# The inverse root of eleven norms in columns: squares as stationary operand, root and reciprocal on 128x4, four matmuls to spread the result over a bank

## The reference

```python
def layer_norm(x, g, b):                       # "a" (512 channels) and "x" (1024) in both layers
    mu = jnp.mean(x32, axis=-1, keepdims=True)
    var = jnp.mean(jnp.square(x32 - mu), axis=-1, keepdims=True)
    y = (x32 - mu) * lax.rsqrt(var + LN_EPS)
    return y * g + b

def rms_norm(x, g):                            # "q" (384), "kv" (256) in both layers; n0, n1, nf (1024)
    return x32 * lax.rsqrt(jnp.mean(jnp.square(x32), axis=-1, keepdims=True) + RMS_EPS) * g

a = jax.nn.silu(layer_norm(a, ln_a_g, ln_a_b))                     # branch A, behind its convolution
q = jnp.einsum("bsr,rk->bsk", rms_norm(q_lat, q_norm_g), w_uq)     # branch C
kv = jnp.einsum("bsr,rk->bsk", rms_norm(kv_lat, kv_norm_g), w_ukv)
return layer_norm(DEEPNORM_ALPHA * x + gate[:, None, :] * out, ln_g, ln_b)   # the end of a layer
```

## Time and profile before

| | us |
|---|---|
| median of 3 executions | 2508.64 (2507.86 to 2511.62) |
| profiled execution, whole | 2511.03 |
| its span on the core | 2509.2 |
| PE busy in it | 2302.8 (92%) |
| VectorE, GpSimd, ScalarE busy | 1454.2, 1070.8, 858.9 |
| mean granted clock of PE | 0.963 of 2.4 GHz |

### The profile page before, as it was taken

How to read it: one execution, slowest core, us unless ns; L and a number is a source line. 1 busy time by engine, 2 the same in 40 slices (tenths; PEclk the granted TensorE clock), 3 DMA queues, 4 the chain that set the end, 5 groups by cost and what they waited for, 6 DMA issues and landing times.

```text
span 2509.2 us, 30799 instructions
## 1 busy us (share of the span) xinstructions
PE 2302.8 (92%) x10776; PEld 1869.3 (74%) x10776; DVE 1454.2 (58%) x2336; ACT 858.9 (34%) x1394; POOL 1070.8 (43%) x1276
## 2 busy tenths in 40 slices
PE   6799899999799989999967989888999999899997
PEld 3587777888568777788746878777778778688875
DVE  5889976432478997632268373654766666423311
ACT  2332234222433233422244233333443443333211
POOL 1555435565246543555414342442343443344333
PEclk9999999999899999999988999999999999999999
DMA  8343324443223222333412222222243242122221
GB/s 294 120 143 110 109 89 139 146 155 118 93 97 111 91 80 78 112 126 107 136 30 86 76 89 86 74 91 98 84 143 112 82 143 81 58 70 73 76 67 67
DMA packets 93203, 259.80 MB, mean 104 GB/s; under 512 B 10128, under 2 KB 11536, under 8 KB 92944
## 3 DMA queue, kind: packets, MB, share of 16 engines
q1 hardware_dynamic: 71392, 210.23, 26.4%
q10 hardware_dynamic: 21680, 47.79, 5.3%
HBM read 237.01 MB, written 20.97 MB: 103 GB/s over the span
## 4 chain that ended last, share of the span: by engine, by line
PE 49%; issue 19%; DVE 15%; POOL 13%; ACT 3%; ACTq 1%; POOLq 0%; DMA 0%; DVEq 0%; SPq 0%
PE bank L1852 15%; PE bank L1853 15%; PE bank L1854 15%; POOL t L387 13%; DVE t L1551 4%; DVE t L1348 2%; DVE t L1067 1%; DVE t L1063 1%; PE bank L1935 1%; DVE t L1126 1%; PE bank L2212 1%; PE bank L1922 1%; DVE t L1548 1%; DVE t L1071 1%; POOL t L404 0%
## 5 line engine op out<-in xcount | busy, mean ns | idle before, releaser
L387 POOL TENSOR_TENSOR t<-t,t 128x256 fp32r<-128x256 f32 x1224 | 1030.2, 872 | 1270.1 <-ACT t L423 1269.7
L1852 PE MATMUL bank<-t,t 128*128 128x512 f32 (+2 forms) x3072 | 1196.9, 390 | 96.2 <-POOL t L387 26.9
L1853 PE MATMUL bank<-t,t 128*128 128x512 f32 (+2 forms) x3072 | 1167.8, 380 | 0.0
L1854 PE MATMUL bank<-t,t 128*128 128x512 f32 (+2 forms) x3072 | 1165.5, 379 | 0.0
L1852 PEld LDWEIGHTS bank<-t,t 128*128 128x128 f32 x3072 | 593.8, 193 | 229.7 <-DVE t L1063 22.9
L1853 PEld LDWEIGHTS bank<-t,t 128*128 128x128 f32 x3072 | 593.4, 193 | 108.5 <-issue 5.0
L1854 PEld LDWEIGHTS bank<-t,t 128*128 128x128 f32 x3072 | 591.1, 192 | 109.0
L423 ACT ACTIVATE t<-t 128x1024 fp32r<-128x1024 f32 x306 | 321.5, 1054 | 248.4 <-PE bank L1854 193.5
L1126 DVE SCALAR_TENSOR_TENSOR t<-t,t,t 128x512 f32<-128x512 f32 x168 | 162.8, 982 | 119.1 <-DMA t<-w_ada 96.2
L1348 DVE SCALAR_TENSOR_TENSOR t<-t,t,t 128x512 f32<-128x512 f32 x240 | 201.7, 840 | 6.7
L1067 DVE SCALAR_TENSOR_TENSOR t<-t,bank 128x512 f32<-128x512 f32 x112 | 76.7, 684 | 186.3 <-PE bank L1854 88.9
(11 more groups left out here) (229 smaller groups left out, 1685.8 us busy)
## 6 DMA issues: line engine op xcount, KB each, us to landing
t<-blocks SPq DMA_DIRECT2D x306, 512.0 KB, 3.7
t<-w_ada SPq DMA_DIRECT2D x144, 256.0 KB, 2.7
t<-w_ada SPq DMA_DIRECT2D x20, 512.0 KB, 11.6
xm_park<-t ACTq DMA_DIRECT2D x16, 384.0 KB, 2.3
s_park<-t ACTq DMA_DIRECT2D x16, 384.0 KB, 2.3
t<-xm_park ACTq DMA_DIRECT2D x16, 384.0 KB, 4.6
t<-s_park ACTq DMA_DIRECT2D x16, 384.0 KB, 5.0
xc_park<-t ACTq DMA_DIRECT2D x16, 256.0 KB, 2.0
```

Source lines behind the costliest of these rows:

```text
L387: low = pool.tensor_tensor(w_lo[slot][:, part], w_raw[slot][:, part], w_hi[slot][:, part].bitcast(F32), ALU.subtract)
L1852: pe.matmul(out, wh, xh, start=start, stop=False)
L1853: pe.matmul(out, wh, xl, start=False, stop=False)
L1854: return pe.matmul(out, wl, xh, start=False, stop=stop)
```

## The change

In the eleven norms the squares become the stationary operand and a column of ones the moving one. A matmul with 128 tokens of a square tile as its weights then gives the sum of each of these tokens in a partition of its own, one column; four of them a tile fill 128x4 of a bank. A matmul with zeros writes these four columns first. ScalarE takes the root of 128x4 and VectorE its reciprocal in `rstd`. Four matmuls, with a column of `rstd` broadcast to 128x128 as weights and the identity moving, write the 512 values into all partitions of a bank, and VectorE's multiplies read that bank. Where the root needs another table than what stands before it, a root of one spare column stands ahead of the squares (`root_ahead`). In a, `merge_gate(0, 0)` now stands behind the root; n0's sums go to bank 4 in place of 5.

```diff
+            def root_ahead():                       # ScalarE: ahead of the squares of a, x, n1, nf
+                act.activation(spare[:, 0:1], eps_rms[:], ACT.Sqrt).then_inc(act_done, a())
+
+            def column_std(bank, n, eps, ready, label):
+                act.wait_ge(pe_done, P(*ready))
+                act.activation(rstd[:], banks[bank][:, 0:4], ACT.Sqrt, bias=eps[:], scale=1.0 / n).then_inc(act_done, a(*label))
...
+                root_ahead()
                 for j in range(NA):
...
+                column_std(3, WA, eps_ln, (l, "a_sq", NA - 1), (l, "a_std"))
                 merge_gate(0, 0)
-                act.wait_ge(pe_done, P(l, "a_sq", NA - 1))
-                act.activation(tmp[2][:], banks[3][:], ACT.Sqrt, bias=eps_ln[:], scale=1.0 / WA).then_inc(act_done, a(l, "a_std"))
                 merge_gate(0, 1)
...
+            def column_rstd(std, label):            # VectorE
+                wa(*std)
+                dve.reciprocal(rstd[:], rstd[:]).then_inc(dve_done, d(*label))
...
             def x_norm(l, j):
-                dve.tensor_tensor(x[:, j, :], x[:, j, :], tmp[2][:], ALU.mult).then_inc(dve_done, d(l, "x_norm", j))
+                dve.tensor_tensor(x[:, j, :], x[:, j, :], banks[5][:], ALU.mult).then_inc(dve_done, d(l, "x_norm", j))
...
                 rotate(tmp[2][64:96, :], banks[1], l, "k_rope")
+                column_rstd((l, "kv_std"), (l, "kv_rstd"))
                 products(B_UQ(l))
...
+            def sum_columns(bank, tile, n, j, label):           # PE
+                if j == 0:
+                    pe.matmul(banks[bank][:, 0:4], ident[:], zeros[:], start=True, stop=False)
+                for t in range(4):
+                    mm = pe.matmul(banks[bank][:, t:t + 1], tile[:, 128 * t:128 * (t + 1)], ones[:, 0:1], start=False, stop=(j == n - 1 and t == 3))
+                mm.then_inc(pe_done, p(*label))
+
+            def spread_rows(bank, ready, label):
+                pe.wait_ge(dve_done, Dn(*ready))
+                for t in range(4):
+                    mm = pe.matmul(banks[bank][:, 128 * t:128 * (t + 1)], rstd[:, t:t + 1].to_broadcast([128, 128]), ident[:], start=True, stop=True)
+                mm.then_inc(pe_done, p(*label))
...
                 for j in range(3):
                     pe.wait_ge(act_done, A(l, "q_lat_sq", j))
-                    sum_rows(banks[2], tmp[j % 2][:], 3, j, (l, "q_sq", j))
+                    sum_columns(2, tmp[j % 2], 3, j, (l, "q_sq", j))
...
+                spread_rows(3, (l, "q_rstd"), (l, "q_rows"))
                 pe.wait_ge(act_done, A(l, "kv_lat", 0))
                 u_chunk(banks[1], B_KR(l), (l, "k_rope"))
...
+                    if h == 0:                      # behind the first q head
+                        spread_rows(6, (l, "kv_rstd"), (l, "kv_rows"))
...
-                    sum_rows(banks[3], tmp[j % 2][:], NA, j, (l, "a_sq", j))
+                    sum_columns(3, tmp[j % 2], NA, j, (l, "a_sq", j))
+                pe.wait_ge(act_done, A(l, "exp", 31))
+                spread_rows(4, (l, "a_rstd"), (l, "a_rows"))
                 merge(0, 1)
...
-                    sum_rows(banks[3], tmp[j % 2][:], KT, j, (l, "x_sq", j))
+                    sum_columns(3, tmp[j % 2], KT, j, (l, "x_sq", j))
+                spread_rows(5, (l, "x_rstd"), (l, "x_rows"))
...
             context_tile(1)
-            norm_sums(range(KT), S, ("n0",), bank=5)
+            norm_sums(range(KT), S, ("n0",), bank=4)
+            spread_rows(6, ("n0", "rstd"), ("n0", "rows"))
...
             norm_sums(range(KT), S, ("n1",))
+            spread_rows(2, ("n1", "rstd"), ("n1", "rows"))
...
             norm_sums(range(KT), S, ("nf",), f_s)
+            spread_rows(2, ("nf", "rstd"), ("nf", "rows"))
```

More of the change, by code:

```diff
@@ L179, in program @@
         mx, nb, ri = (at(o_small + 128 + 32 * i, [128, 2]) for i in range(3))
-        rs = at(o_small + 224, [128, 4])
-        o_small += 256
+        rs, rstd, zeros, spare = (at(o_small + 224 + 32 * i, [128, 4]) for i in range(4))
+        o_small += 352
         o_acc = o_small
@@ L752, in _ @@
                     norm_squares(x, [j - 1], S, ("n0",), ready=lambda j: (act_done, A(L1 - 1, "y", j)))
-            norm_std(S, KT, ("n0",), bank=5)
+            column_std(4, D, eps_rms, ("n0", "sq", KT - 1), ("n0", "std"))
             for j in range(KT):
@@ L988, in _ @@
                         split_to(B_W(h) + j // 2 + 1 + RING)
+            root_ahead()
             norm_squares(x, range(KT), S, ("n1",), ready=lambda j: (dve_done, Dn("x2", MH - 1, j)))
-            norm_std(S, KT, ("n1",))
+            column_std(3, D, eps_rms, ("n1", "sq", KT - 1), ("n1", "std"))
             for j in range(KT):
@@ L1188, in norm_recip, with norm_parts @@
                 wd()
-            def norm_parts(tiles, hi, lo, js, cols, shift, label, tmp=tmp):
+            def norm_parts(tiles, hi, lo, js, cols, shift, label, rows, tmp=tmp):
                 def low_part(j):
@@ L1199, in norm_parts @@
                         wd(*label, "uL", j - 2)
-                    dve.scalar_tensor_tensor(tmp[3 + j % 2][:, 0:cols], tiles[:, j, :], scale1[:, 1, j:j + 1], tmp[2][:, 0:cols],
+                    dve.scalar_tensor_tensor(tmp[3 + j % 2][:, 0:cols], rows, scale1[:, 1, j:j + 1], tiles[:, j, :],
                                              ALU.mult, ALU.mult).then_inc(dve_done, d(*label, "scaled", j))
@@ L1445, in _ @@
                         .then_inc(dve_done, d(l, "a_cent", j))
-                wa(l, "a_std")
-                dve.reciprocal(tmp[2][:], tmp[2][:]).then_inc(dve_done, d())
-                wd()
+                column_rstd((l, "a_std"), (l, "a_rstd"))
+                wp(l, "a_rows")
                 for j in range(NA):
-                    dve.tensor_tensor(a_acc[:, j, :], a_acc[:, j, :], tmp[2][:], ALU.mult).then_inc(dve_done, d(l, "a_norm", j))
+                    dve.tensor_tensor(a_acc[:, j, :], a_acc[:, j, :], banks[4][:], ALU.mult).then_inc(dve_done, d(l, "a_norm", j))
                 products(B_Y(l) + 1)
@@ L1502, in _ @@
                         norm_recip(CTX, ("nc",), ctx_tmp)
-                        norm_parts(ctx_x, cH2, cL2, range(KT), CTX, lambda i: ada[:, 3, i:i + 1], ("nc",), ctx_tmp)
+                        norm_parts(ctx_x, cH2, cL2, range(KT), CTX, lambda i: ada[:, 3, i:i + 1], ("nc",), ctx_tmp[2][:], ctx_tmp)
                 wp(l, "x_mean")
@@ L1507, in _ @@
                         .then_inc(dve_done, d(l, "x_cent", j))
[L1508 to L1511, removed]
+                column_rstd((l, "x_std"), (l, "x_rstd"))
+                wp(l, "x_rows")
             for j in range(KT):
@@ L1515, in _ @@
             norm_scales(2, 0)
-            norm_recip(S, ("n0",))
-            norm_parts(x, uH, uL, range(KT), S, lambda j: ada[:, 2, j:j + 1], ("n0",))
+            column_rstd(("n0", "std"), ("n0", "rstd"))
+            wp("n0", "rows")
+            norm_parts(x, uH, uL, range(KT), S, lambda j: ada[:, 2, j:j + 1], ("n0",), banks[6][:])
             wd()
@@ L1788, in _ @@
             norm_scales(4, 1)
-            norm_recip(S, ("n1",))
-            norm_parts(x, uH, uL, range(KT), S, lambda j: ada[:, 4, j:j + 1], ("n1",))
+            column_rstd(("n1", "std"), ("n1", "rstd"))
+            wp("n1", "rows")
+            norm_parts(x, uH, uL, range(KT), S, lambda j: ada[:, 4, j:j + 1], ("n1",), banks[2][:])
             def fu_parts(g):
@@ L1838, in _ @@
                                          ALU.mult, ALU.add).then_inc(dve_done, d("x3", j))
-            wa("nf", "std")
-            dve.reciprocal(f_rstd[:], f_rstd[:]).then_inc(dve_done, d())
-            wd()
+            column_rstd(("nf", "std"), ("nf", "rstd"))
+            wp("nf", "rows")
             for j in range(KT):
-                dve.scalar_tensor_tensor(x[:, j, :], x[:, j, :], V("norm_f", 0, j), f_rstd[:], ALU.mult, ALU.mult)\
+                dve.scalar_tensor_tensor(x[:, j, :], banks[2][:], V("norm_f", 0, j), x[:, j, :], ALU.mult, ALU.mult)\
                     .then_inc(dve_done, d("out", j))
@@ L1934, in norm_sums @@
                     pe.wait_ge(act_done, A(*label, "sq", j))
+                    if cols == S:
+                        sum_columns(bank, tmp[j % 2], KT, j, (*label, "sq", j))
+                        continue
                     pe.matmul(banks[bank][:, 0:cols], ones[:], tmp[j % 2][:, 0:cols], start=(j == 0), stop=(j == KT - 1))\
```

30 lines of the change are left out of this document (13 added, 17 removed).

## The result

| | before | after |
|---|---|---|
| median, us | 2508.25 (2506.60 to 2511.62, 4 executions) | 2530.80 (2527.77 to 2533.01, 4 executions) |
| ratio | | 1.008, 95% interval 1.0069 to 1.0092 |
| profiled span, us | 2509.2 | 2529.6 |
| mean granted clock | 0.963 | 0.945 |

The account below looks back on a forecast made before the run. TensorE was taken as the bound, busy 2302.8 of 2509.2 us. The terms 3.3 + 4.6 + 5.6 + 5.2 + 9 - 1 made +26.7 us, 2535 on the median, range 2512 to 2545.

Parts of the forecast that it names:

- The clock: In the sums, one-column matmuls drop PE to 1.2 GHz: 0.21 us an instruction, 1.68 a tile; case chance 0.72.
- x of layer 0: Layer 0's output norm: slow sums outweigh the shorter tail, multiply at 666.7 against 663.40, +3.3 us.
- Case W: Rival for all norms: the clock holds, one-column matmuls keep it up; -6.95 us, 2501.7, chance 0.13.
- q and kv: Attention norms: layer 0 zero, between +3 and -3; layer 1 loses a 1.90 us wait, -1 us.
- the two a norms: Norm a, both layers: spread ahead of merge(0,1), whose wide reciprocal was hidden; +4.5 us each, +9.
- One argument for the fall: Stretch from 867.40 in the earlier trace: 9 matmuls after the drop, 27 before, taken as a clock fall.
- nf: Norm nf, squares from 2488.55: same form as n1, output right behind, +5.2 us.
- x of layer 1 with n0: Layer 1's output norm and the norm behind it: +1.8 us for x, +4.6 for both.
- n1: Norm n1: early root 1.6 us, slow tiles 5.4, tail -1.35; +5.6 us.
- the early root: At n1: costs PE 1.6 us ahead of the squares, takes 1.3 from the end; moved, not saved.
- PE's idle time before: Whole kernel before: about 196 us in which PE has nothing, the only place an edit gains time.
- The zeroing: In x of layer 0: first wait and zeroing matmul together 0.4 us ahead of the sums.

Follow-up runs that it names:

- e1_wide: The changed kernel with each column matmul of the sums streaming 128 columns of ones and the zeroing matmul 512 wide; 2503.11 us, ratio 0.9963 to the kernel before.
- e9_no_zeroing: e1_wide without its zeroing matmuls and nothing else; 2493.02 us, ratio 0.9921 to the kernel before.
- e10_qkv_only: The kernel before with 128 columns streamed and no zeroing, in the norms q and kv alone; 2503.73 us, ratio 0.9971.
- e5_best: e1_wide without zeroing, with the spread of a behind merge(0,1) and no early root at n1; 2489.59 us, ratio 0.9917 to the kernel before.
- e6_a_old: e5_best with norm a in its form before the change; 2488.98 us, ratio 0.991 to the kernel before.
- e4_no_ahead: The changed kernel without the early root at n1; 2529.46 us, one execution.
- e7_filler512: The changed kernel with a 508-column matmul of constants added ahead of each tile's one-column matmuls, and the wide zeroing; 2553.47 us, one execution.

## Why the prediction was right

**The clock** was the step that carried it, and it held: slots of 0.11 us at full clock and 0.21 at half, 13.79 us for 64 instructions where 8 x 1.68 = 13.4 was worked out, spread 2.08 (2.1), tail 2.9 with hand-overs (2.75), multiply at 665.85, in a trace that was 0.7 ahead there (666.7), x of layer 0 +3.15 (+3.3). e1_wide shows the cause. The Trainium skill (TensorE: Matmul & The Clock Gate, Part 1) lets the clock follow how busy PE is; here PE was busy 13.96 us of 14.20 and had 0.50, so busy by the profile's account is not what keeps it. Case W was the sum for a clock that holds, -6.95. That e1_wide, where it mostly does, has -7.5 is luck: W had no 512-wide zeroing, and e1_wide pays 10.5 us for it. Without it e9_no_zeroing has -18. W gave q and kv 2 us, where e10_qkv_only has 7.4, and charged the two a norms 4, where e5_best and e6_a_old differ by 0.6. One argument for the fall was weak: the 27 matmuls ahead of the drop in the earlier trace rows are mostly narrow and the 9 behind it mostly 512 columns wide, so their counts say nothing of the clock; its own column in those rows does.

**The size**, 22.5 for 26.7 (20.7 in the matched traces), hides terms that were off in both directions: nf, a, x of layer 1 with n0, and q and kv came out 1 to 4 us lower each, n1 2.3 higher. That the sum came so near is in part luck. nf was +1.7 and not +5.2: the clock fell only in the fifth tile, and the 1.5 us for the early root were wrong there, since ScalarE was waiting for PE's products anyway and did the load in that wait:

```profile
2497.45 1.28 ACT L473 ACT_TABLE_LOAD   x1
...
2507.25 0.20 ACT L473 ACTIVATE t<-t 128x1 f32<-128x1 f32 x1 [8.52 <-PE bank L1865]
```

n1 was +7.9 and not +5.6: the load exposed ahead of the squares leaves PE idle 3.26 us in place of 1.75, the sums are at half clock from the first tile, and the first products behind it run slower for longer (1.7 us). The two a norms were +4.6 and not +9, as waits further on gave back 3.8 and 1.1 us. x of layer 1 and n0 were +2.9 and not +4.6, with the parts the other way round: the sums of x took 11.9 us for 7.6 (+4.3, where 3.2 was booked without a working; eight tiles at 0.83 are 6.6) and those of n0 10.9 for 9.9 (+1.0, where 4 was booked), as the clock was at full for the first part of both. Against that stand 3.5 us in stretches that the sum didn't name. PE's idle time before was put at 196 us; by the earlier trace rows it is 206, and nothing hangs on it.

a of layer 0 shows the wait that the spread brings:

```profile
395.38 3.76 PE L1940 MATMUL bank<-t,t 128*128 128x1 f32 x32
...
399.17 0.26 ACT L478 ACTIVATE t<-bank,t 128x4 f32<-128x4 f32 x1 [1.14 <-PE bank L1940]
...
399.47 0.18 DVE L1198 RECIPROCAL t<-t 128x4 f32<-128x4 f32 x1 [6.66 <-ACT t L478]
399.79 2.04 PE L1947 MATMUL bank<-t,t 128*128 128x128 f32 x8 [0.66 <-DVE t L1198]
...
401.49 0.77 PE L1863 MATMUL bank<-t,t 128*128 128x512 f32 x1
```

The sums end at 399.14 in 3.76 us, still at full clock; PE stands 0.66 us for root and reciprocal, spreads for 2.04, and the first matmuls of merge(0,1) take 0.63 each in place of 0.39. So at a of layer 0 the sums themselves cost nothing, and the clock came down behind them. At a of layer 1 it came down within them, and with the zeroing they take 4.98 us for 3.78.

**The early root** was told as moved, not saved. In the earlier trace rows the sums end at 2146.25 and the load at 2146.37: it cost 0.12 us there. The sum booked its 1.6 us (1.6 + 5.4 - 1.35) and so had the right sign, but the words that it takes 1.3 from the end were wrong, as e4_no_ahead shows.

**q and kv** came out at -2.2 against -1 (the start's -1.4 and layer 1's -0.8), and e10_qkv_only gives the form more than this where the clock is held.

**The zeroing** of four columns was priced at about 0.4 us with the first wait of x of layer 0, and took 0.45 there (648.72 to 649.17). It is not needed: the first matmul into the bank can start it, as in e9_no_zeroing.

## What to carry to other kernels

Where every matmul has its own weight load, one column costs nearly the same as 128 (0.113 and 0.119 us at full clock), but in this kernel rows of one-column ones let PE's clock fall though PE never stood still; make such matmuls as wide as the slot allows, and look at the granted clock of the stretch, not at PE's busy share. Shrinking a tail between engines (4.5 us to 2.0 here) is worth its length only where nothing lay beside it: at a it was worth nothing. A table load behind the last square is free as long as the sums of the last tiles outlast it; put ahead of the squares it was free only where ScalarE waited anyway, at nf.

## What the runs showed of the hardware

The one-column and the 128-column form take nearly the same slot at full clock (0.113 and 0.119 us on average, in nf of the changed kernel and of e1_wide) and the same at half (0.213, in x of layer 0 of both), so the wide form is all but free in time. With PE busy throughout, the granted clock was 0.50 for 29 us in one norm and 1.00 for 14 us in another, under the same sequence of 508-column and one-column matmuls; in a third norm of the same kernel it rose from 0.50 to 1.00 under it (e7_filler512). Streaming constants and streaming data made no difference to the clock (2553.47 and 2552.48, one execution each). Ahead of n1 the same wide sums began at half clock behind 3.26 us without work for PE (e9_no_zeroing) and at full clock behind 1.75 (e5_best). Column matmuls need no zeroed bank: one start for the bank and none for its other columns was enough. Zeroing all 512 columns of it eleven times cost 10.5 us (e1_wide against e9_no_zeroing).
